# A hybrid attention layer on one core: the first weight block split piece by piece, the second unit's lower products last, tile 2 of x turned in two pieces

## The reference

```python
h = rmsnorm(x, norm_pre_g)                      # 512 x 1024
u = einsum('bsd,de->bse', h, w_in)              # 1024 x 4096 weights
dq, dk, dv, dg, mq, mk, mv, mg = split(u, ...)  # eight groups of 512 columns
# differential attention on dq, dk, dv; block attention on mq, mk, mv
y = concat([a_out * silu(dg), b_out * silu(mg)]) @ w_out
out = x + rmsnorm(y, norm_post_g)
```

## Time and profile before

| | |
|---|---|
| median of 3 runs | 258.5 us (258.47 to 259.34) |
| the profiled execution | 258.57 us |
| its span in the profile | 256.8 us |
| PE busy in the span | 248.0 us, 97% |
| DVE, ACT, POOL busy | 69%, 56%, 13% |
| share of the chain that ended last: PE, DMA, ACT, DVE | 89%, 5%, 2%, 1% |
| mean granted clock of PE | 0.993 of full speed |

### The profile page before, as it was taken

One profiled execution on the slowest core, in us unless ns is written; L12 is line 12 of the kernel. 1 busy time (PEld: TensorE's weight loads), 2 busy tenths in 40 slices (PEclk: granted clock), 3 DMA queues, 4 the chain that ended last, 5 costly groups with the idle time before them and its releaser, 6 DMA issues.

```text
span 256.8 us, 4437 instructions
## 1 busy us (share of the span) xinstructions
PE 248.0 (97%) x1589; PEld 124.2 (48%) x1589; DVE 176.3 (69%) x382; ACT 144.4 (56%) x337; POOL 32.9 (13%) x77
## 2 busy tenths in 40 slices
PE   7899999999999999999999999999999999999991
PEld 7644444444444544545454444454444444554470
DVE  1797675467677798898677767966688885934413
ACT  3987646256355758767475595685557654611110
POOL 2129400000000040050022032000000001011101
PEclk9999999999999999999999999999999999999997
DMA  6979997897217325543424674599619746997422
GB/s 213 400 237 259 237 293 283 259 376 198 69 20 202 93 57 160 137 115 102 130 87 121 119 189 116 123 227 128 163 38 128 154 77 157 224 196 240 123 84 83
DMA packets 59627, 42.47 MB, mean 165 GB/s; under 512 B 45761, under 2 KB 46025, under 8 KB 59605
## 3 DMA queue, kind: packets, MB, share of 16 engines
q1 hardware_dynamic: 59604, 42.19, 63.5%
HBM read 29.04 MB, written 2.13 MB: 121 GB/s over the span
## 4 chain that ended last, share of the span: by engine, by line
PE 89%; DMA 5%; ACT 2%; DVE 1%; POOL 1%; issue 0%; SPq 0%; DVEq 0%; POOLq 0%; ACTq 0%
PE unit_ps L542 72%; PE score_ps L576 6%; PE o_ps L596 5%; PE unit_ps L558 4%; DMA pt<-arena 3%; DMA stage<-in_w_in_dram 2%; PE score_ps L649 1%; PE unit_ps L649 1%; ACT junk L672 1%; ACT w_hi L685 1%; ACT w_hi L686 0%; DVE arena L869 0%; DVE area L968 0%; POOL x_ms L438 0%; ACT area L718 0%
## 5 line engine op out<-in xcount | busy, mean ns | idle before, releaser
L542 PE MATMUL unit_ps<-area,w_hi 128*128 128x512 f16 x256 | 76.2, 379 | 0.0
L542 PE MATMUL unit_ps<-w_hi,area 128*128 128x512 f16 x224 | 70.6, 379 | 1.1 <-DVE w_lo L819 0.8
L726 ACT ACTIVATE arena<-arena,negmax 128x512 f32<-128x512 f32 (+3 forms) x64 | 35.4, 554 | 50.0 <-DVE negmax L895 49.8
L542 PE MATMUL unit_ps<-area,w_lo 128*128 128x512 f16 x128 | 48.5, 379 | 0.0
L542 PE MATMUL unit_ps<-w_lo,area 128*128 128x512 f16 x112 | 42.4, 379 | 0.0
L542 PEld LDWEIGHTS unit_ps<-area,w_hi 128*128 128x128 f16 x256 | 23.9, 98 | 26.5 <-issue 0.8
L542 PEld LDWEIGHTS unit_ps<-w_hi,area 128*128 128x128 f16 x224 | 21.9, 98 | 27.5 <-issue 2.0
L817 DVE SCALAR_TENSOR_TENSOR w_lo<-stage,g_cols,w_hi 128x512 f16<-128x512 f32 x32 | 24.2, 758 | 15.4 <-ACT w_hi L686 15.3
L895 DVE CUSTOM_DVE_ANT_0 arena<-score_ps,strips 128x512 f32<-128x512 f32 (+3 forms) x64 | 28.6, 483 | 8.9 <-PE score_ps L576 8.9
L685 ACT ACTIVATE w_hi<-stage,g_cols 128x512 f16<-128x512 f32 x32 | 22.7, 711 | 9.2 <-DMA stage<-in_w_in_dram 9.1
L819 DVE SCALAR_TENSOR_TENSOR w_lo<-stage,g_cols,w_hi 128x512 f16<-128x512 f32 x32 | 24.8, 776 | 0.0
(11 more groups left out here) (98 smaller groups left out, 342.3 us busy)
## 6 DMA issues: line engine op xcount, KB each, us to landing
stage<-in_w_in_dram SPq DMA_DIRECT2D x32, 512.0 KB, 4.7
stage<-in_w_out_dram SPq DMA_DIRECT2D x8, 512.0 KB, 3.8
arena<-in_x_dram SPq DMA_DIRECT2D x4, 512.0 KB, 8.0
strips<-bias_rows SPq DMA_DIRECT2D x1, 2048.0 KB, 10.8
stage<-in_x_dram SPq DMA_DIRECT2D x4, 512.0 KB, 4.5
out_dram<-area SPq DMA_DIRECT2D x3, 512.0 KB, 3.3
strips<-bias_rows SPq DMA_DIRECT2D x1, 1024.0 KB, 8.6
g_row<-in_norm_post_g_dram SPq DMA_DIRECT2D x1, 512.0 KB, 11.5
```

Source lines behind the costliest of these rows:

```text
L542: last = nc.tensor.matmul(bank, a, b, start=(k == 0 and n == 0), stop=(k == KT - 1 and n == 2))
L726: nc.scalar.activation(probs[:, i % 2, m, 0:n], probs[:, i % 2, m, 0:n], ACT.Exp, bias=negmax[:, i, m:m + 1], scale=-1.0, accum_out=sums[: ...
```

## The change

It has six parts.

- Quarter 0 is split block by block. `split_first(k)` on ACT and DVE handles one block of 512 columns, with the semaphores `first_hi` and `first_lo` for block 0, and the halves of x tile 0 are put between the blocks. PE waits for `first_lo` before block 0 and for `split_lo` before block 1.
- The mean square of the tiles 1 to 3 moves from POOL (L438) to DVE (`x_mean_square`); the power stays on POOL.
- Unit 1 joins the units 2 and 3 in `late_lower_unit`: the products with the upper half of x come first, in two halves of k, and the lower products last. Unit 1 then waits for `ht_hi_ready` first and for `ht_ready` only before its lower products.
- On ACT, `x_hi(1)` comes before `x_square(2)`, and the read-out of unit 0 before `xn_hi(2)`. On DVE, too, the read-out of unit 0 comes before `xn_lo(2)`.
- The upper half of tile 2 is written by ACT in two instructions of 512 columns and turned by two DMA transposes (`turn_x_part`).
- On SP these two transposes stand between load 4 and load 5; before, both transposes of tile 2 stood behind load 5.

```diff
+            def turn_x_part(part):
+                sp.wait_ge(xn_hi_ready, part + 1)
+                ks = slice(part * KT // 2, (part + 1) * KT // 2)
+                sp.dma_start_transpose(ht[:, 0, ks, 2 * P:3 * P], x_halves[:, 0, 0, part * DM // 2:(part + 1) * DM // 2])\
+                    .then_inc(x_turned[0][0] if part else x_turned_part, 16)
...
             load_quarter(4)
+            for part in range(2):
+                turn_x_part(part)
             load_quarter(5)
-            for h in range(2):
-                turn_x(2, h)
+            turn_x(2, 1)
             load_quarter(6)
...
+                    pool.wait_ge(x_mean, 1)
                 else:
-                    nc.gpsimd.tensor_scalar(x_ms[:, t:t + 1], x_sq[:, t:t + 1], NORM_EPS, 1.0,
-                                            ALU.add, ALU.mult).then_inc(x_mean, 1)
-                pool.wait_ge(x_mean, t + 1)
+                    pool.wait_ge(x_ms_ready, t)
...
-                pe.wait_ge(split_lo, 4 * g + q + 1)
+                if (u, q) == (0, 0):
+                    pe.wait_ge(first_lo, 1)
+                else:
+                    pe.wait_ge(split_lo, 4 * g + q + 1)
                 for k in (2 * q, 2 * q + 1):
+                    if (u, k) == (0, 1):
+                        pe.wait_ge(split_lo, 1)
...
-            def turned_unit(u):
+            def late_lower_unit(u):
...
+                for part in range(2):
+                    if i == 1:
+                        pe.wait_ge(ht_hi_ready, x_count(1))
+                    elif i == 2 and part == 0:
+                        pe.wait_ge(x_turned_part, 16)
+                    else:
+                        pe.wait_ge(x_turned[i - 2][0], 16)
+                    ks = range(part * KT // 2, (part + 1) * KT // 2)
+                    for b in (w_hi, w_lo):
+                        for k in ks:
+                            nc.tensor.matmul(bank, ht[:, 0, k, rows], b[:, g % 3, k, :],
+                                             start=(k == 0 and b is w_hi), stop=False)
+                if i == 1:
+                    pe.wait_ge(ht_ready, x_count(1))
+                else:
+                    pe.wait_ge(x_turned[i - 2][1], 16)
+                for k in range(KT):
+                    last = nc.tensor.matmul(bank, ht[:, 1, k, rows], w_hi[:, g % 3, k, :], start=False,
+                                            stop=(k == KT - 1))
...
+            def split_first(k):
+
+                src = stage[:, 0, k * WIDTH:(k + 1) * WIDTH]
+                nc.scalar.activation(w_hi[:, 0, k, :], src, ACT.Copy, scale=g_cols[:, k:k + 1])\
+                    .then_inc(split_hi if k else first_hi, 1)
+
             x_square(0)
-            split(0)
+            act.wait_ge(w_loaded[0], 16)
+            act.wait_ge(g_scaled, 1)
+            split_first(0)
             x_hi(0, 0)
+            split_first(1)
             x_hi(0, 1)
             split(1)
             x_square(1)
             split(2)
             split(3)
+            x_hi(1)
             x_square(2)
-            x_hi(1)
+            unit(0)
             xn_hi(2)
             x_square(3)
...
+            split_first(0)
             x_lo(0, 0)
+            split_first(1)
             x_lo(0, 1)
             split(1)
+            x_mean_square(1)
             x_norm(1)
             split(2)
             split(3)
             x_lo(1)
+            x_mean_square(2)
+            unit(0)
             xn_lo(2)
+            x_mean_square(3)
```

More of the change, by code:

```diff
@@ L259, in bass_hymba_diff_moba_layer @@
         split_lo = sem("split_lo")
+        first_hi = sem("first_hi")
+        first_lo = sem("first_lo")
         consts_ready = sem("consts_ready")
@@ L272, in bass_hymba_diff_moba_layer @@
         x_turned = [[sem(f"x_turned{t}_{h}") for h in range(2)] for t in range(2, TILES)]
+        x_turned_part = sem("x_turned_part")
+        x_ms_ready = sem("x_ms_ready")
         unit_done = sem("unit_done")
@@ L354, in store_rows @@
                 sp.dma_start(out_v[t], y_sb[:, t % 2, :]).then_inc(stored[t % 2], 16)
+            def turn_x_part(part):
[3 more added lines that the diff above has]
+                    .then_inc(x_turned[0][0] if part else x_turned_part, 16)
             def turn_x(t, h):
-                sp.wait_ge(xn_lo_ready if h else xn_hi_ready, t - 1)
+                sp.wait_ge(xn_lo_ready if h else xn_hi_ready, t - 1 if h else t)
                 sp.dma_start_transpose(ht[:, h, :, t * P:(t + 1) * P], x_halves[:, t - 2, h, :])\
@@ L521, in unit_quarter @@
                         for t in range(2, need + 1):
+                            pe.wait_ge(x_turned[t - 2][0], 16)
                             pe.wait_ge(x_turned[t - 2][1], 16)
@@ L551, in turned_unit @@
                 rows = slice(i * P, (i + 1) * P)
-                pe.wait_ge(unit_freed, u - 1)
+                if u >= 2:
+                    pe.wait_ge(unit_freed, u - 1)
                 pe.wait_ge(split_lo, 4 * (g + 1))
[L554 to L559, removed]
+                for part in range(2):
[17 more added lines that the diff above has]
+                                            stop=(k == KT - 1))
                 last.then_inc(unit_done, 1)
@@ L611, in _ @@
                     x_transposes(1)
[L612 to L615, removed]
+            for u in range(1, TILES):
+                late_lower_unit(u)
             for u in range(TILES, FIRST_UNITS):
@@ L682, in split @@
                 if g < len(GROUPS):
-                    if n == 0:
-                        act.wait_ge(g_scaled, 1)
                     nc.scalar.activation(w_hi[:, g % 3, k, :], src[:, 0, :], ACT.Copy, scale=g_cols[:, k:k + 1])
@@ L752, in xn_hi @@
                 act.wait_ge(x_rstd_ready, t + 1)
-                nc.scalar.activation(x_halves[:, t - 2, 0, :], x_sb[:, t, :], ACT.Copy,
-                                     scale=x_rstd[:, t:t + 1]).then_inc(xn_hi_ready, 1)
+                n = DM // (2 if t == 2 else 1)
+                for lo in range(0, DM, n):
+                    nc.scalar.activation(x_halves[:, t - 2, 0, lo:lo + n], x_sb[:, t, lo:lo + n], ACT.Copy,
+                                         scale=x_rstd[:, t:t + 1]).then_inc(xn_hi_ready, 1)
             def x_square(t):
@@ L777, in _ @@
                     split(n)
-                unit(u)
+                if u > 0:
+                    unit(u)
                 if u == 2:
@@ L862, in unit, with x_mean_square @@
                 ins.then_inc(unit_freed, 1)
+            def x_mean_square(t):
+                dve.wait_ge(x_squared, t + 1)
+                nc.vector.tensor_scalar(x_ms[:, t:t + 1], x_sq[:, t:t + 1], NORM_EPS, 1.0, ALU.add,
+                                        ALU.mult).then_inc(x_ms_ready, 1)
             def x_norm(t, part=0):
@@ L872, in xn_lo @@
             def xn_lo(t):
-                dve.wait_ge(xn_hi_ready, t - 1)
+                dve.wait_ge(xn_hi_ready, t)
                 nc.vector.scalar_tensor_tensor(x_halves[:, t - 2, 1, :], x_sb[:, t, :], x_rstd[:, t:t + 1],
@@ L982, in _, with split_first @@
             x_norm(0, 1)
-            split(0)
+            def split_first(k):
+                dve.wait_ge(split_hi if k else first_hi, 1)
+                src = stage[:, 0, k * WIDTH:(k + 1) * WIDTH]
+                nc.vector.scalar_tensor_tensor(w_lo[:, 0, k, :], src, g_cols[:, k:k + 1], w_hi[:, 0, k, :],
+                                               ALU.mult, ALU.subtract).then_inc(split_lo if k else first_lo, 1)
+            split_first(0)
             x_lo(0, 0)
+            split_first(1)
             x_lo(0, 1)
             split(1)
+            x_mean_square(1)
             x_norm(1)
```

## The result

The changed kernel takes 264.51 us (median of 6, 262.26 to 266.07), the kernel before 258.71 (median of 6, 258.35 to 259.46). The ratio is 1.0213, 95% interval 1.0177 to 1.0249: slower by 5.8 us. The direction was right, the size was not: 1.8 us were forecast, 5.8 came, outside the range. The profiled execution took 265.76 us, 7.2 us more than that of before; it is the second slowest of the six, so what its rows show is more than the 5.8 us of the medians.

The account below looks back on a forecast made before the run. PE was taken to bound the kernel. An earlier run (-0.29) and a new gap before unit 3 (+2.08) gave +1.8 us on 258.57, so 260.4 us; its own range was 259.9 to 261.8, the overall range 258.6 to 262.3.

Parts of the forecast that it names:

- the sum: At unit 3's start: 0.29 us gained by the earlier run, 2.08 us lost in a new gap, together +1.8 us.
- Part 5: SP's queue: quarter 5 behind both pieces of tile 2, half a transpose 0.7 us of issue, quarter 6 issued 1.5 us later.
- The landing: Quarter 6's load, issued at 22.15, lands between 26.15 and 27.85; 26.5 was taken.
- A rival with a chance of 0.03: PE's clock falls in the gap before unit 3; one unit at half rate costs 5.18 us more, about 267; chance 0.03.
- Part 2: Mean square on DVE, power on POOL: tile 1's scaling starts 0.29 us earlier, or a 0.09 us loss with the long power.
- part 4: ACT and DVE read out unit 0 before tile 2's halves: first piece about 0.9, second and lower half about 1.5 us later.

Follow-up runs that it names:

- the last two small gains: Two runs against the kernel before: read-out of unit 1 ahead of quarter 6's split, 0.9978; block-by-block split and unit 1's order with only tile 1's mean on DVE, 0.9974.

## Why the prediction was wrong

**Right.** PE bounds the kernel, only two places can move its end, and the one that does is the start of unit 3, behind quarter 6, which SP issues too late. Blocks 4 to 7 began at 14.74 (forecast 14.82), ACT read out unit 0 at 17.53 (17.6) and wrote the pieces from 18.02 (18.2), the first transpose went out at 18.76 (18.85). POOL's power for tile 1 took 0.56 us, the short one of its two prices. PE's first product came at 9.14 and not at 10.01, as tile 0 and with it the warm-up came 0.7 us earlier; that was worth nothing, as said, because PE waited again before block 2.

**Where it failed: the sum.** Its term for quarter 6 was mis-sized twice, in the issue and in the landing, and the fall of the clock, which the sum left out, came on top.

| term | forecast | measured |
|---|---|---|
| quarter 6 issued | 22.15 | 23.31 |
| issue to landing | 4.35 (bounds 4.0 and 5.7) | 6.8 |
| from ACT's split to unit 3 | 3.35 | 3.44 |
| unit 3 starts | 29.85 | 33.58 |
| unit 3 takes | 5.2 | 6.9 |

*Part 5, the transpose of half the columns.* I took 0.7 us of issue where the row gave 1.3 for a whole one, and said that the price would drop out "unless both take 1.3". Both took about 1.3 (1.29 and 1.25), a case that the sum did not carry. The lower half, ready at 20.66, stood behind them and quarter 5 until 22.04. The late issue is 1.16 of the missing 3.7 us at unit 3. The pair of runs with quarter 5 in front sizes a second issue at 1.6 us, within 0.4 to 2.8.

*The landing.* I let it range by the two loads of before and judged by what is ahead of quarter 6 in the queue. The prediction named the extra 512 KB of quarter 5 and priced it at 0.35 us. The runs show 0.8 to 2.8 us for a queue with quarter 5 in the stretch and tile 3's transposes behind, 2.8 in the profile of the changed kernel, and in one run 0.5 with those transposes held back. The bound from the rows was not a bound, since no row of before showed a load with another one issued 1.9 us ahead of it and a transpose between. The landing is the largest of the three, 2.45 of the 3.7 us at unit 3.

*The clock.* A rival with a chance of 0.03 came true beside the late quarter 6, with another price: the gap was 5.2 us and not 2.1, the clock fell as unit 3 began and was back by 38 us, so 1.7 us and not 5.2. The prediction held that a gap of 2.1 us should pass, from a stretch at 1.00 and one at 0.50; the stretch between them, which it left out, has 0.69, so the clock of the kernel before fell within 3 us of its last product at 251.2:

```profile
253.00:254.00 1.00, 0.00 (x0) 0.00 (x0) 1.00 (x2) 0.00 (x0) 0.00 (x0) 0.69 0.03 8
```

With the long landing of its own bounds (+3.15, a gap of 3.4 us) the clock was in reach, and 0.03 was too little. By the rule of the Trainium skill named beside that rival (TensorE: Matmul & The Clock Gate, on the HAM clock gate), idleness throttles and activity releases; the trace agrees, and its clock rows are 0.50 from 34 to 37 us. It goes with the scatter of the executions: of the six, the two with the highest mean clock (0.998 and 0.996) took 262.3 and 263.2 us, the four at 0.993 or less 264.5 to 266.1. Only one of the six was profiled, so that the rest of the scatter is that of the landings is likely and not shown.

**Missed in its weight.** The prediction had tile 2's factor at 17.85 instead of 16.7 and called the read-out of unit 0 what delays the halves. Undoing the read-out changed little; the mean square on DVE is what holds the factor. Part 2 counted only tile 1's gain, 0.29 us, which came, and part 4 carried the later factor without setting it against part 2: 1.1 us at a place without slack.

**Where the 2.13% lie.** Going from the changed kernel to the one with quarter 5 in front: 1.1%. From there to one piece: 0.6%. With the read-out and squares in the order of before too, 0.4% remain (1.0037). The means of tiles 2 and 3 back on POOL turn this into 0.9974, 0.6% less, which is more than remained. Each step is a difference of two ratios with 0.3 to 0.5% of uncertainty.

**Open.** Why another load ahead, with transposes around it, holds a load's last bytes, at 46 GB/s, is not settled, nor why the same queue order gave 5.6 us in one profile and 6.8 in another, nor how much of it is due to the transposes behind. Whether the last two small gains are real side by side is open too.

## What to carry to other kernels

A queue entry that waits for a late producer turns the transfers behind it into a burst, and landing times taken from a calm stretch do not bound those in a burst. Before an instruction is moved to a faster engine, look at what it will stand behind there: 0.14 us of work in DVE's list cost tile 2 more than a microsecond that an idle POOL did not. When a start has no slack, find the second gate close behind the first, as here tile 3's transpose behind the read-out, before pricing a fix.

## What the runs showed of the hardware

A DMA transpose of 128 x 512 elements took as long to issue on SP as one of 128 x 1024: 1.25 to 1.30 against 1.23 to 1.35 us where the queue did not hold the larger one up (up to 5.55 us where it did). It landed in 2.5 us against 3.1 or more.

The landing of a 512 KB load depends on what shares its stretch: 3.9 to 4.1 us in seven profiles with the load before it issued at least 8 us earlier, 4.8 to 6.8 us in six with that load 1.9 us ahead and transposes on both sides. With the transposes behind held back it was 4.5 us, in one profile. In the changed kernel's stretch the 16 DMA engines moved 46 GB/s for 2.2 us with packets outstanding (share 1.44). The kernel before has such a stretch too, half as long and with a share of 0.66:

```profile
25.70:26.70 1.00, 1.00 (x6) 0.47 (x5) 0.62 (x1) 0.82 (x2) 1.00 (x6) 1.00 0.66 46
```

PE's granted clock was 0.50 for about 3.4 us after an idle stretch of 5.2 us, and 24 products of 512 columns took 6.9 us in place of 5.2. With PE busy in 3.3 us of the gap it stayed at 1.00.
